# Copying each tile's normed rows to two PSUM banks for VectorE's first-table products

## The reference, cut to what matters

```python
def chunk(xc):                                  # 128 tokens, normed
    q = (xc @ w_q).reshape(PEER_CHUNK, PEER_HEADS, 2, PEER_HALF)
    s = jnp.einsum('thid,hikd->thik', q, sub_keys)
    ...                                         # top 16 of 16 x 16 sums, 8 heads
    gate = jax.nn.softmax(top_s, axis=-1)
    u = u_emb[eidx]                             # 128 chosen rows per token
    hid = jax.nn.gelu(jnp.einsum('td,thkd->thk', xc, u))
    wgt = gate * hid
    return jnp.einsum('thk,thkd->td', wgt, v_emb[eidx])
```

## Time and profile before

| | us |
|---|---|
| median of 3 runs | 3625.47 |
| lowest and highest run | 3599.13, 3627.65 |
| span of the profiled execution | 3615.4 |

### The profile page before, as it was taken

The page is one execution under the profiler, slowest core; times in us unless marked ns, Lnnn a source line. Parts: engine busy times, 40 slices in busy tenths (PEclk is TensorE's granted clock), DMA queues, the critical chain, the costliest instruction groups (busy, mean ns, idle before and its releaser), DMA issues.

```text
span 3615.4 us, 31605 instructions
## 1 busy us (share of the span) xinstructions
PE 2906.2 (80%) x10954; PEld 1575.0 (44%) x10954; DVE 2183.0 (60%) x4395; ACT 609.2 (17%) x1471; POOL 1765.2 (49%) x1556
## 2 busy tenths in 40 slices
PE   5999999876798988967776667898998957666767
PEld 3557587555344456462222222345645722222223
DVE  1422178887775787286666664576626676666643
ACT  1320021223104200111111111110015111111111
POOL 0000013325564675057777777546300277777776
PEclk8999999786899999989999999899999989999999
DMA  7664468889898899489999999898942589999999
GB/s 246 215 211 154 159 232 304 297 291 347 338 338 314 311 397 377 175 315 391 372 368 369 373 369 405 310 332 330 338 159 86 199 318 369 367 368 361 371 377 360
DMA packets 402489, 1113.00 MB, mean 308 GB/s; under 512 B 37155, under 2 KB 91619, under 8 KB 401436
## 3 DMA queue, kind: packets, MB, share of 16 engines
q0 software_dynamic: 223024, 811.71, 60.1%
q1 hardware_dynamic: 179308, 299.27, 23.6%
HBM read 1106.57 MB, written 4.29 MB: 307 GB/s over the span
## 4 chain that ended last, share of the span: by engine, by line
PE 47%; DMA 19%; POOL 16%; DVE 9%; issue 7%; ACT 2%; SPq 0%; DVEq 0%; POOLq 0%; ACTq 0%
PE PS L532 35%; POOL ring L1158 15%; DMA ring<-in_peer_v,eidx 12%; PE PS L615 9%; DMA wring<-in_w_in 3%; DVE ring L1559 3%; DMA ring<-in_peer_u,eidx 2%; ACT work L1173 1%; PE PS L857 1%; PE PS L636 1%; DVE work L1647 1%; DMA wring<-in_w_mod 1%; DVE work L1641 1%; PE PS L865 1%; PE PS L540 0%
## 5 line engine op out<-in xcount | busy, mean ns | idle before, releaser
L1158 POOL DMA_INDIRECT ring<-in_peer_u,eidx x768 | 855.7, 1114 | 1259.1 <-DVE work L2097 361.9
L615 PE MATMUL PS<-ring,diag 128*128 128x512 f32 x2112 | 1031.9, 617 | 429.5 <-DMA ring<-in_peer_v,eidx 313.1
L1559 DVE SCALAR_TENSOR_TENSOR ring<-ring,xn_peer 128x1024 f32<-128x1024 f32 x768 | 931.2, 1222 | 500.5 <-DMA ring<-in_peer_u,eidx 498.3
L1158 POOL DMA_INDIRECT ring<-in_peer_v,eidx x768 | 899.5, 1171 | 429.8 <-issue 157.8
L615 PEld LDWEIGHTS PS<-ring,diag 128*128 128x128 f32 x2112 | 369.2, 192 | 1080.7 <-issue 520.9
L532 PE MATMUL PS<-wring,xnT 128*128 128x512 f32 (+2 forms) x1600 | 683.0, 589 | 22.4 <-issue 12.3
L532 PE MATMUL PS<-xnT,wring 128*128 128x128 f32 (+1 forms) x2896 | 492.8, 333 | 46.9 <-DMA wring<-in_w_in 37.8
L532 PEld LDWEIGHTS PS<-xnT,wring 128*128 128x128 f32 x2896 | 444.6, 196 | 94.1 <-DMA wring<-in_w_in 42.2
L532 PEld LDWEIGHTS PS<-wring,xnT 128*128 128x128 f32 x1600 | 306.7, 195 | 391.3 <-issue 382.2
L1201 ACT ACTIVATE diag<-const,small 128x128 f32<-128x128 f32 x528 | 203.3, 400 | 970.7 <-PE PS L615 947.0
L532 PE MATMUL PS<-wring,work 128*128 128x512 f32 (+2 forms) x768 | 316.9, 574 | 24.0 <-ACT work L1173 8.3
(11 more groups left out here) (194 smaller groups left out, 1680.2 us busy)
## 6 DMA issues: line engine op xcount, KB each, us to landing
wring<-in_w_in SPq DMA_DIRECT2D x128, 1024.0 KB, 7.6
wring<-in_w_mod SPq DMA_DIRECT2D x48, 1024.0 KB, 8.5
wring<-in_peer_wq SPq DMA_DIRECT2D x24, 1024.0 KB, 6.3
wring<-in_ab_w_in SPq DMA_DIRECT2D x13, 1024.0 KB, 17.4
wring<-in_conv_out_w SPq DMA_DIRECT2D x12, 1024.0 KB, 10.9
wring<-in_w_out SPq DMA_DIRECT2D x12, 1024.0 KB, 8.7
ring<-in_peer_u,eidx POOLq DMA_INDIRECT x768, 6.4
ring<-in_peer_v,eidx POOLq DMA_INDIRECT x768, 6.5
```

The costliest lines, as they stand in the source:

```text
L615: ins = pe.matmul(PS[:, b + c, :], diag[:, state["summed"] % ND, :], ring[:, m % NG, 512 * c:512 * c + 512], start=(k == SUMS[r, t][0]), s ...
L1158: pool.indirect_dma_start(ring[:, m % NG, :], None, tables[kind], bass.IndirectOffsetOnAxis(ap=eidx[:, r % 2, t, k:k + 1], axis=0))\
L1559: v.scalar_tensor_tensor(out=slot, in0=slot, scalar=1.0, in1=xn_peer[:, t, :], op0=ALU.mult, op1=ALU.mult, accum_out=hid[:, t, k:k + 1]).t ...
```

## The change

Before the first first-table row of each tile and run, VectorE copies the tile's normed rows from `xn_peer` into two PSUM banks (`put_row_input`), waits for that copy, and the products read them there (`row_input`). The banks are 6 and 7 in run 0, 0 and 1 for tile 0 and 2 and 3 for tile 1 in runs 1 and 2. Rows 80 to 127 of run 0's tile 1 go on reading `xn_peer`, since banks 6 and 7 hold a sum by then; TensorE waits before that sum's first row until VectorE has finished row 79. To keep the banks free, the attentions "ab" and "c" turn over `[4, 5]`, the products of the first block and of mixer 1 over banks 0 to 5, the front of run 1 over 2 to 5 and that of run 2 over 2 to 7.

```diff
--- before.py
+++ after.py
@@ -469,6 +469,11 @@
 
         LAST_M = [k for k in OWN[0, 0] if k < b][-1]
 
+        def row_input(r, t):
+
+            b = 2 * t if r else 6
+            return PS[:, b:b + 2, :].rearrange("p b n -> p (b n)")
+
         def used_wait(m):
             by_pe, n = ORDER[m]
             return slot_summed if by_pe else slot_used, n + 1
@@ -584,7 +589,8 @@
 
             def attention(s, units, scores, turns, values, between=None):
 
-                state["banks"] = [4, 5] if s in SUMS_PER_UNIT else [4, 5, 6, 7]
+                held = s in ("ab", "c", 1)
+                state["banks"] = [4, 5] if held else [4, 5, 6, 7]
                 late = VALUES_AFTER if s in RUN else 2
                 for u in range(len(units) + late):
                     if u < len(units):
@@ -599,7 +605,7 @@
                         values(u - late)
                     if u < len(units):
                         sum_rows(SUMS_PER_UNIT.get(s, 0))
-                state["banks"] = list(range(6)) if s in SUMS_PER_UNIT else list(range(8))
+                state["banks"] = list(range(6 if held else 8))
 
             def sum_rows(n):
 
@@ -608,6 +614,8 @@
                     r, _, t, k = ITEMS[m]
                     b, _ = sums(r, t)
                     if k == SUMS[r, t][0]:
+                        if r == 0:
+                            pe.wait_ge(slot_used, PLACE[0, "u", 1, U1_EARLY - 1] + 1)
                         take([b, b + 1], ("acc", r, t))
                     pe.wait_ge(*at("diag", r, t, k))
                     pe.wait_ge(g_landed[m % NG], 16 * (m // NG + 1))
@@ -912,6 +920,8 @@
                             release(*blocks)
 
             def peer_front(r):
+                state["banks"] = state["banks"][2:] if r else state["banks"][:6]
+
                 def turned(t):
                     pe.wait_ge(*at("xn", ("p", r), t))
                     turn(xn_peer[:, t, :], ("xnT", ("p", r), t), KD)
@@ -965,6 +975,8 @@
             peer_front(1)
             for t in range(T):
                 sum_rows(len(SUMS[1, t]))
+                for b in range(2 * t, 2 * t + 2):
+                    state["user"][b] = ("row_input", 1, t)
             state["banks"] = list(range(8))
             mixer(2)
             peer_front(2)
@@ -1541,6 +1553,14 @@
 
             rows_at = {"next": 0, "chosen": 0, "weighted": 0, "pace": 0.0, "due": 0.0, "per_product": 0, "upto": len(DVE_ITEMS)}
 
+            def put_row_input(r, t):
+
+                v.wait_ge(*(at("read", "sub", r, T - 1, GROUPS - 1) if t else at("read", "xnT", ("p", r), T - 1, 1)))
+                if r == 0 and t:
+                    v.wait_ge(slot_used, PLACE[0, "u", 0, NSEL - 1] + 1)
+                v.tensor_copy(row_input(r, t), xn_peer[:, t, :]).then_inc(*step("dve", "row_input", r, t))
+                v.wait_ge(*at("row_input", r, t))
+
             def expert_rows(n):
 
                 for _ in range(n):
@@ -1553,10 +1573,12 @@
                         return
                     rows_at["next"] += 1
                     slot = ring[:, m % NG, :]
+                    if (kind, k) == ("u", 0):
+                        put_row_input(r, t)
                     v.wait_ge(g_landed[m % NG], 16 * (m // NG + 1))
                     if kind == "u":
 
-                        v.scalar_tensor_tensor(out=slot, in0=slot, scalar=1.0, in1=xn_peer[:, t, :], op0=ALU.mult,
+                        v.scalar_tensor_tensor(out=slot, in0=slot, scalar=1.0, in1=xn_peer[:, t, :] if r == 0 and t and k >= U1_EARLY else row_input(r, t), op0=ALU.mult,
                                                op1=ALU.mult, accum_out=hid[:, t, k:k + 1]).then_inc(slot_used, 1)
                     elif kind == "v" and k == OWN[r, t][0]:
                         v.tensor_scalar(acc[:, :], slot, weights_of(r, t)[:, k:k + 1], None, ALU.mult).then_inc(slot_used, 1)
@@ -1579,6 +1601,7 @@
                         h = H[RUN[r][1]][:, t, :]
                         v.tensor_tensor(h, h, acc[:, :], ALU.add).then_inc(*step("dve", "h_peer", r, t))
                         same("dve", "read", "acc", r, t)
+                        same("dve", "read", "row_input", r, t)
                         v.wait_ge(L.sem["dve"], L.count["dve"])
 
             def rows_upto(r, kind, t, k):
```

## The result

The changed kernel takes 3515.62 us (median of 4 runs, 3513.02 to 3518.39); the kernel before, 3619.91 (4 runs, 3599.13 to 3627.65; three of them are those of the table further up). The ratio is 0.9723 with a 95% interval of 0.9693 to 0.9753. The profiled execution has a span of 3513.2 us, 102 us less than 3615.4.

The account below looks back on a forecast made before the run. GpSimd's gathers, prolonged by VectorE's two-SBUF-operand products, were taken to bound the expert stretches of runs 1 and 2; -47 - 63 - 6 + 4 + 4 = -108 us turned the 3615.4 us span into 3507, median 3518, range 3478 to 3590.

Parts of the forecast that it names:

- The operand pair: First-table products: 720 of 768 read one operand from PSUM, no longer holding up gathers; saves 47, 63 and 6 us.
- the change doesn't do what it says: Rival: a PSUM operand with accumulated output still holds up gathers; 3627 us, chance 0.13 shared with the DMA rival.
- 1.30 us a gather: Expected pace in runs 1 and 2, above 1.277 because eight slots last 10.2 us against 8.7 to land and use.
- the floor of 410 GB/s: DMA's limit on gathers, 1.277 us each, taken from 47 gathers in 2180 to 2240 us of the kernel before.
- GpSimd never waits for a free slot: Reading of run 1's expert stretch before: GpSimd is the bound, each gather costing its duration plus 0.31 us.
- Run 0: In 600 to 1100 us most of the gathers' 57 us excess hides under waits for VectorE; saving 6 us, 0 to 16.
- Copies, banks, waits: Cost of the change's six copies, 4 us, and of all banks plus TensorE's new wait, 4 us.
- The handover in the "ab" attention: VectorE's output read precedes the exponentials' end by 0.58 us, covering transposes on two banks; 0, up to 10 us.
- The product's own time: First-table products on VectorE take no longer with a PSUM operand: 0, bounds -5 to +5 us.
- DMA is the bound already: Rival: in runs 1 and 2 relieving GpSimd moves nothing; 3627 us, chance 0.13 shared with the ineffective-operand rival.
- Half way: Rival: TensorE's second-table chain or VectorE's choice takes over, 1.36 us a gather; 3574 us, chance 0.13.
- Slower: Rival: first-block attention becomes serial, up to 64 us; with the main gain missing 3690 us, chance 0.04.

Follow-up runs that it names:

- e1: Changed kernel with its copies, waits and banks, but every first-table product reads the normed rows in SBUF again: 3625.5 us, ratio 1.0029 to the kernel before.
- e4: Changed kernel with the product's operands swapped, PSUM rows first and ring slot second: 3518.53 us in one run.
- e12: Changed kernel with ten slots in runs 1 and 2, the SBUF tiles of normed rows serving as two more: 3510.62 us, ratio 0.9713.
- e5: Changed kernel with each gather moving half a row, same number of gathers, output not the reference's: 3401.99 us in one run.
- e8: Kernel before with seven slots in use, GpSimd also waiting for the slot seven gathers back: 3689.13 us, against 3629.88 for the kernel before on that chip.
- e2: Changed kernel with run 0 as in the kernel before (SBUF operand, full bank lists around the first block): 3517.53 us, ratio 0.9724.
- e6: Kernel before with each gather moving half a row, output not the reference's: 3616.24 us, against 3629.88 for the kernel before on that chip.
- the variants: Changed kernel with run 0's late rows in PSUM too, with ten slots, and with both: 3631.1, 3635.55 and 3634.91 us; kernel before there 3664.84.
- e3: Changed kernel with products of odd k reading SBUF, only even k PSUM: 3551.31 us, ratio 0.9821.

## Why the prediction was right

*Total.* The sum was -108 us for the span; it measured -102. Runs 1 and 2 gave 10 us less than forecast, and all the rest 4 us more. The median came to 3515.6 where 3518 was said, and that it is nearer than the span (3513.2 for 3507) is luck: 10 us were added for the distance of median and span, which came out as 2.4. The lower end of 3478 also leaves out the 2 us that the copies were to cost at the least.

*The operand pair* was forecast from two places of the timeline, the second without an accumulated output. e1 shows that the operand is the whole gain, e4 that its order doesn't matter; the rival that the change doesn't do what it says is out. The Trainium skill (SBUF — State Buffer, "Who interferes with whom") says the same: a VectorE instruction with two SBUF inputs contends with a GpSimd instruction that reads SBUF, one with at most one doesn't, outside VectorE's two-port modes. This case agrees, 1.36 against 0.94 us. The exception may show here too, in few gathers: the `tensor_scalar` of line 1562 has one SBUF tensor and takes only 0.75 us for 1024 columns, and both gathers of before that start inside one take 1.44 and 1.45 us and end 0.81 us after it. This case goes beyond the page in one thing. The page reports that `tensor_tensor` did not hold up a DMA issued from GpSimd; here an indirect one, which reads its row numbers from SBUF, is held up by `tensor_tensor` too: the 22 gathers of before that start well inside one of line 1641 on two SBUF tensors of `work` have a mean of 1.16 us and end 0.81 us after it, the 13 inside a `max8` of line 2099 have 0.938. What GpSimd reads at that moment was not tested.

*1.30 us a gather.* Measured 1.304 (600 / 460) and 1.311 (640 / 488). Runs 1 and 2 were to save 47 and 63 us; they saved 43.6 and 56.6. The pace is right, and the floor of 410 GB/s was read rightly from the 60 us where the kernel before reached it: the changed kernel has 404 and 400 over its runs. The reason given for the 0.03 us above the floor was a tighter ring, and that was at most partly so. Two more slots gave back 10 us in two runs, less than half of it (e12); with half the bytes it is 1.26 us (e5). VectorE at the floor would have been busy 67 to 70% of the time by its own rows, not "near 75%"; it is 65 to 68%.

*"GpSimd never waits for a free slot"*, and so slots don't matter before, was too strong. In runs 1 and 2 of before 45 of 1010 gathers start within 0.35 us of the moment their slot comes free, against 260 after, and one slot less costs 34 us of waits and 22 us of longer gathers (e8). The budget of 8.7 us out of 10.2 used medians; in run 1 landing takes up to 9.2 us, not 6.4.

*Run 0* was to give 6 us. e2, which leaves out its relief and its costs, has the same time; 53 us of stalls went, and what came of it is below what these runs can tell. That most of the stalls hide, as forecast, is shown; the 6 us are not.

*Copies, banks, waits*: 8 us were said for the change without its operand, and e1 has 10 us (3 to 18 by its interval). The copies were 1.21 us each (six, 1212 ns mean):

```profile
L1561 DVE COPY PS<-xn_peer 128x1024 f32<-128x1024 f32 x6 | 7.3, 1212 | 0.0
```

The handover in the "ab" attention cost next to nothing (0.45 us ahead of one weight load), as said, but my reading of what covers it was wrong. In the trace of after:

```profile
635.26 2.08 PE L688 MATMUL PS<-work 64*128 64x256 f32 x8
...
636.33 0.40 ACT L1273 ACTIVATE work<-work,small 128x128 f32<-128x128 f32 x1 [3.09 <-DVE small L1775]
...
636.74 0.42 DVE L1664 TENSOR_TENSOR work<-PS,small 128x256 f32<-128x256 f32 x1
...
637.27 1.59 PE L705 MATMUL PS<-const,work 128*128 128x128 f32 x8
```

The transposes start as TensorE's own scores end (637.34), while the exponentials that I had named go on behind them. VectorE's read ends at 637.16, 0.11 us ahead of the transposes, 0.58 before. The slip from which this would cost something is smaller than I said, and in the "c" attention it came, twice: TensorE waits there between the two banks' transposes until VectorE has read the output, the sign that the prediction named as wrong.

```profile
863.11 1.11 PE L705 MATMUL PS<-const,work 128*128 128x128 f32 x4 [0.50 <-DVE work L1664]
...
898.59 1.12 PE L705 MATMUL PS<-const,work 128*128 128x128 f32 x4 [1.58 <-DVE work L1664]
```

Neither before nor e2 has such a wait. It is 2.1 us of TensorE's time, and the 0 to 10 us said for the banks allow for it.

*The product's own time*: 1217 ns with PSUM, 1222 without, as the rows of before had it. The 62 cycles between the fixed parts that the Trainium skill (VectorE: DVE Perf Modes, "The TRN2 errata") gives for a PSUM and an SBUF source are not borne out.

*Rivals.* "DMA is the bound already" is excluded by e6, on its chip: half of the bytes, no faster in runs 1 and 2. But it became the bound after the change. On the slower chip the variants gain only 0.8%; that DMA was nearly the bound there already is likely by its 372 GB/s, but not shown, since no trace of the kernel before comes from that chip. The 358 GB/s of the Trainium skill (SBUF — State Buffer, "Summary: rules for kernel authors") is below what every kernel with whole rows moved in 1700 to 2100 us: 363 GB/s (e1) to 406 (e12), 371 and 372 on the slower chip. "Half way" is the case that e3 shows in small.

*Slower*, the serial attention, did not come: with the waits above the whole time up to run 1 is 1550.8 us, 1552.0 before.

## What to carry to other kernels

A GpSimd that issues gathers back to back is slowed by VectorE instructions beside it that read two SBUF tensors: a gather that starts inside one ended 0.81 us after it here. Put one operand in PSUM if two banks can be spared, and read the effect from the gather's duration, not from the DMA share. A DMA share near 1 did not mean a bound: the test is whether half of the bytes are faster. A second sign is the rate in short slices: pinned at one value (405 to 412 GB/s after), or touching it and falling back (before). A stall removed where the stalled engine waits for another anyway brings little, however many microseconds it has (53 in run 0, with nothing to be seen in the total).

## What was not expected of the hardware

- Moving fewer bytes made the kernel before slower in its gather-bound stretches: with even landings of 3.7 us the second-table gathers run into products (118 of 134 take over 1 us, against 70 of 140), and in 1700 to 2100 us one goes out every 1.49 us, not 1.42.
- Chips differ in what DMA delivers to the same code: 372 GB/s against 405 over 400 us, and 3665 against 3614 to 3630 us for the kernel before. Why, and why GpSimd's waits there come some 25 us apart, stays open.
